# Feed-forward down products of the middle steps in pairs of 64-row matmuls

## The chip, the cores and the metric

One core of a Trainium2 chip runs the whole program. The metric is device time in microseconds (us) of one execution, as the median over the runs shown. The core has a matmul engine (TensorE, PE in the profile, with its weight loads shown apart as PEld), a vector engine (DVE), a scalar engine (ACT), GpSimd (POOL) and queues that issue DMAs.

## The reference, cut to what matters

Two transformer blocks follow each other on 256 tokens of width 1024, all in fp32. They hold five feed-forward parts (swiglu), one in the first block and four in the second:

```
def _swiglu(h, w_gate_up, w_down):
    g, u = jnp.split(h @ w_gate_up, 2, axis=-1)
    return (jax.nn.silu(g) * u) @ w_down
```

The hidden width is 2816, so that the down product sums over 2816 hidden features for each of the 256 x 1024 outputs.

## The kernel before, in words

All products run on TensorE in fp32r, a rounded form of fp32. To keep accuracy each operand is held as a high and a low part (whi and wlo of the weights, st_hi and st_lo or hid_hi and hid_lo of the activations), and `product` (lines 661 to 665) makes three matmuls of each: high x high, high x low, low x high, all added in one PSUM bank. A matmul is written `128*128 128x512` in the profile: 128 rows (the summed dimension) and 128 columns of the stationary operand, then the moving operand with its 512 columns.

Weights come in units of 128 x 2048. A DMA puts a unit into `raw`, ACT rounds it into `whi` (line 1415), DVE subtracts to get `wlo` (line 1984), and TensorE uses it; each of the three buffers is a ring of three. TensorE counts the units that it has finished in `w_used`, and ACT waits for that count before it fills a place again.

`swiglu` on TensorE (line 1042) takes the hidden width in FSTEPS = 11 steps of 256 features. A step has three units: two for gate and up, one for down. The order on TensorE is the gate and up products of step i (`gate_up`, 48 matmuls into banks 4 and 5), then the down products of step i-1 (`down`, line 1083). Meanwhile ACT and DVE make silu, the hidden values and their turned and split form `hid_hi` and `hid_lo`, 128 features by 2 by 256 tokens. `down` waits for `hid_ready` and for its weight unit, and calls `down_block` (line 1069) for each of two token blocks tb. A block loops over two output halves h and two feature groups f; each (tb, h) has its own bank, and all eleven steps add to the same four banks 0 to 3. A step has 2 x 2 x 2 x 3 = 24 down matmuls, each 128*128 with 512 moving columns.

`down` runs for steps 0 to 8 of each feed-forward part: once before the loop (line 1106) and eight times in `pe.Fori` (line 1107). Steps 9 and 10 are written out after the loop and call `down_block` themselves. So `down` runs 9 x 5 = 45 times in the program.

The kernel has other matmuls that use 64 rows: `scores2` (line 1254) in the second attention computes heads in pairs, the even head on rows 0 to 63 and the odd one on rows 64 to 127, in plain fp32, where the profile shows two matmul instructions for each call. Its semaphore `even_scored` (lines 1253 and 1259) keeps two halves off one bank. `cmp_scores` (line 1273) does the same with 16 moving columns. `values2` (lines 1320 to 1330) uses 64 stationary columns. The product for the attention gates ("g2") is in fp32r with 48 stationary columns.

Of the kernel before, what the change touches and what calls it, by code (L numbers as in the profile page):

```python
# [30 lines left out]
P = 128  # L31
# [5 lines left out]
FSTEPS = DFF // FC  # L37
# [40 lines left out]
def build(nc, A, out):  # L78
    ctx = ExitStack()
    with ctx:  # L80
        def sb(name, shape, dt=F32):
            return ctx.enter_context(nc.sbuf_tensor(name, shape, dt))

        def sem(name):
            return ctx.enter_context(nc.semaphore(name))
# [9 lines left out]
        hid_hi = sb("hid_hi", [P, 2, S], F32R)  # L95
        hid_lo = sb("hid_lo", [P, 2, S], F32R)
# [127 lines left out]
        w_used = sem("w_used")  # L224
# [28 lines left out]
        factor_ready = sem("factor_ready")  # L253
        factor1_ready = sem("factor1_ready")
        even_scored = sem("even_scored")
        prob_end_ready = sem("prob_end_ready")
        cmp_p_ready = sem("cmp_p_ready")
        act_step = sem("act_step")
# [93 lines left out]
        def at(base, i=0):  # L352

            return base + RING * i, base % RING, base // RING + i
# [143 lines left out]
        def bank(key):  # L498
            return ps[:, use[key][0], :]
# [15 lines left out]
        def is_full(key):  # L515
            return bank_full[use[key][0]], 1
# [137 lines left out]
        def _(pe):  # L654
# [6 lines left out]
            def product(o, a, b, start, stop):  # L661

                pe.matmul(o, a[0], b[0], start=start, stop=False)  # L663
                pe.matmul(o, a[0], b[1], start=False, stop=False)  # L664
                return pe.matmul(o, a[1], b[0], start=False, stop=stop)  # L665
# [163 lines left out]
            for h in range(2):  # L829
                pe.matmul(gain_rows(h), ones, gb[0:1, 1, 512 * h:512 * h + 512], start=True,  # L830
                          stop=True).then_inc(gain_ready, 1)
# [12 lines left out]
                      stop=True).then_inc(*is_full("rows"))  # L844
            room("kidx")
            u = first["kidx"]
            features(u, [(0, bank("kidx")[:, 0:S])]).then_inc(w_used, 1)
            room("qidx")
            u = first["qidx"]
# [3 lines left out]
            for tb in range(2):  # L853
                mm = pe.transpose(bank("widx")[:, 4 * tb:4 * tb + 4], widxT[64:68, tb * P:tb * P + P],
                                  ident[64:68, 64:68])
            mm.then_inc(*is_full("widx"))
            room("kv")
            u = first["kv"]
# [5 lines left out]
            for j in range(2):  # L864
                mm = pe.matmul(bank(("dots", 0))[:, S * j:S * j + S].rearrange("p (a b) -> p a b", a=2),
                               qidx[:, j, 0:P], kidx[:, :, 0:P], start=True, stop=True)
            mm.then_inc(*is_full(("dots", 0)))
            for j in range(2):
                room(("dots", 1 + j))
                pe.matmul(bank(("dots", 1 + j)), qidx[:, j, P:2 * P], kidx[:, :, :].rearrange("p a b -> p (a b)"),  # L870
                          start=True, stop=True).then_inc(*is_full(("dots", 1 + j)))
# [12 lines left out]
            for tb in range(2):  # L884
                mm = pe.transpose(bank("vT")[:, tb * P:tb * P + P], v1T[:, tb * P:tb * P + P], ident)
# [8 lines left out]
            for j in range(2):  # L894
                room(("pool", j))
                for g in (2 * j, 2 * j + 1):
                    src = (winA, winB)[g % 2]
                    mm = pe.matmul(bank(("pool", j))[:, (g % 2) * S:(g % 2 + 1) * S], poolw[:, g, :],
                                   src[:, g, 16:272], start=True, stop=True)
# [142 lines left out]
            def swiglu(n, name=None, src=None, ahead=None, middle=None, behind=None, between=None):  # L1042
                u0 = first["ffn", n]
                up = [("up", n, tb) for tb in range(2)]
                ykeys = [[("y", ("ffn", n), tb, h) for h in range(2)] for tb in range(2)]

                def gate_up(i, base, j, between=None):
                    for half in range(2):
                        u, s, _ = at(base + half, j)
                        pe.wait_ge(wlo_ready, u + 1)  # L1050
                        w = [x[:, s, :].rearrange("p (k c) -> p k c", k=4) for x in (whi, wlo)]
                        for tb, key in enumerate(up):
                            if half == 0:

                                b, c = use[key]
                                pe.wait_ge(bank_read[b], c + i)
                            for k in range(4):
                                mm = product(bank(key), [x[:, 4 * half + k, tb * P:tb * P + P] for x in (st_hi, st_lo)],
                                             [x[:, k, :] for x in w], half == 0 and k == 0, half == 1 and k == 3)
                            if half == 1 and tb == 0:  # L1060
                                mm.then_inc(*is_full(up[0]))
                        mm.then_inc(w_used, 1)
                        if half == 0 and between is not None:
                            between()

                def down_block(w, x_hi, x_lo, tb, start=False, end=False, ahead=None):
                    for h in range(2):
                        for f in range(2):
                            if ahead is not None and (h, f) == (1, 1):
                                ahead()  # L1070
                            mm = product(bank(ykeys[tb][h]), [x[:, f, tb * P:tb * P + P] for x in (x_hi, x_lo)],
                                         [x[:, f, 512 * h:512 * h + 512] for x in w], start and f == 0,
                                         end and f == 1)
                        if end and (tb, h) != (1, 1):
                            mm.then_inc(*is_full(ykeys[tb][h]))
                    return mm

                def down_weights(base, j):
                    u, s, _ = at(base, j)
                    pe.wait_ge(wlo_ready, u + 1)  # L1080
                    return [x[:, s, :].rearrange("p (k c) -> p k c", k=2) for x in (whi, wlo)]

                def down(i, base, j, start=False):

                    pe.wait_ge(hid_ready, hid_count(n, i))
                    w = down_weights(base, j)
                    down_block(w, hid_hi, hid_lo, 0, start)
                    down_block(w, hid_hi, hid_lo, 1, start).then_inc(w_used, 1)

                def turn_last(tb):  # L1090
                    key = ("hid_last", n, tb)
                    pe.wait_ge(*read(up[tb], FSTEPS - 1))
                    room(key)
                    for f in range(2):
                        mm = pe.transpose(bank(key)[:, f * P:f * P + P], hidden[:, tb, f * P:f * P + P], ident)
                    mm.then_inc(*is_full(key))

                by_block([(u0 + half, 4, 512, 4 * half, [bank(key) for key in up], up, half == 0, half == 1)
                          for half in range(2)], st=name, src=src, middle=middle)
                if behind is not None:  # L1100
                    behind()

                gate_up(1, u0 + 2, 0, between=between)
                for key in (k for pair in ykeys for k in pair):
                    room(key)
                down(0, u0 + 4, 0, start=True)
                with pe.Fori(2, FSTEPS - 1) as i:
                    gate_up(i, u0 + 2, i - 1)
                    down(i - 1, u0 + 4, i - 1)


                i = FSTEPS - 1
                gate_up(i, u0 + 2, i - 1)
                turn_last(0)
                pe.wait_ge(hid_ready, hid_count(n, i - 1))
                w_before = down_weights(u0 + 4, i - 1)
                down_block(w_before, hid_hi, hid_lo, 0)
                turn_last(1)
                w_last = down_weights(u0 + 3 * FSTEPS - 1, 0)
                last = [x[:, 8:10, :] for x in (st_hi, st_lo)]  # L1120
                pe.wait_ge(*read(("hid_last", n, 0)))
                down_block(w_last, *last, 0, end=True)
                down_block(w_before, hid_hi, hid_lo, 1).then_inc(w_used, 1)
                pe.wait_ge(*read(("hid_last", n, 1)))
                down_block(w_last, *last, 1, end=True, ahead=ahead).then_inc(w_used, 1)
# [8 lines left out]
            for j in range(2):  # L1134
                room(("wsT", j))
                for q in range(4):
                    mm = pe.transpose(bank(("wsT", j))[:, q * P:q * P + P], ws[:, 4 * j + q, :], ident)
                mm.then_inc(*is_full(("wsT", j)))
            for j in range(2):
                room(("bs", j))  # L1140
                for q in range(4):
                    v = vec[:, V_BS + 4 * j + q:V_BS + 4 * j + q + 1]
                    mm = pe.matmul(bank(("bs", j))[:, q * P:q * P + P], view(v, (0, P)), ident, start=True, stop=True)
# [79 lines left out]
            w = weights(first["g2"], KD, 48)  # L1223
            for k in range(KD):
                if k % 4 == 0:
                    wait_st("ln3", k // 4)
                mm = product(bank("g2")[0:48, 0:S], [x[:, k, :] for x in w], [x[:, 8 + k, :] for x in (st_hi, st_lo)],
                             k == 0, k == KD - 1)
# [108 lines left out]
            for g in range(4):  # L1337
                for f in range(2):
                    mm = pe.matmul(bank("vc")[:, g * 64:g * 64 + 64], cmp_gr[:, f, g, :],
                                   cmp_w2[:, 1, f, 0:64], start=f == 0, stop=f == 1)  # L1340
# [3 lines left out]
            for tb in range(2):  # L1344
                mm = pe.transpose(bank("g2T")[:, 48 * tb:48 * tb + 48], gateT2[0:48, tb * P:tb * P + P],
                                  ident[0:48, 0:48])
# [1619 lines left out]
```

## Time and profile before

| what | value |
|---|---|
| median of 2 runs | 1455.52 us (1455.5 to 1455.54) |
| the profiled execution, its own time | 1458.33 us |
| its span, first to last instruction | 1456.6 us |
| around the span | 1.7 us |
| granted TensorE clock, mean | 0.998 |

The profiled execution is 0.2% longer than the median of the runs shown. PE busy time counts overlapping instructions once, and an instruction's own time holds its way through the array too: back to back matmuls of 0.39 us start 0.23 us apart. What counts for throughput is the distance between starts.

### The profile page before, as it was taken

The numbers are of one execution on the slowest core, as the hardware profiler recorded it, in microseconds if no ns is written. First come the engines' busy times: TensorE is split into PE (matmuls) and PEld (weight loads), VectorE is DVE, ScalarE is ACT, GpSimd is POOL, SyncE is SP. The second block draws the span as 40 slices with busy tenths as digits, with TensorE's granted clock in tenths as the row PEclk, the third lists the DMA queues.
The fourth block names the chain that finished last, engine by engine and source line by source line (L and its number), as shares of the span: only waits on it lengthen the run. The fifth ranks groups of instructions, "written<-read, shape, count | busy, mean of one in ns | idle before, by whom it ended". The sixth has DMA issues, their size and how long they took to land.

```text
span 1456.6 us, 20700 instructions
## 1 busy us (share of the span) xinstructions
PE 1438.3 (99%) x7418; PEld 1210.3 (83%) x7418; DVE 1077.1 (74%) x1818; ACT 679.2 (47%) x848; POOL 207.4 (14%) x191
## 2 busy tenths in 40 slices
PE   9999999999999999999999999999999999999997
PEld 7988897888888888889988888888888897788886
DVE  5666766888777887757758887757877777688876
ACT  5346456444444444443434444435444477454342
POOL 1073011200001000300032000201000325510001
PEclk9999999999999999999999999999999999999999
DMA  8753553865656556575577555775556450465561
GB/s 251 255 174 126 203 178 117 295 209 173 198 193 206 197 173 198 177 231 173 169 236 240 201 173 194 238 231 173 173 196 207 150 174 30 139 236 174 183 215 64
DMA packets 198701, 273.94 MB, mean 188 GB/s; under 512 B 9585, under 2 KB 158193, under 8 KB 198386
## 3 DMA queue, kind: packets, MB, share of 16 engines
q1 hardware_dynamic: 194130, 256.10, 53.6%
q0 software_dynamic: 4368, 16.78, 3.2%
q8 instruction: 39, 0.64, 0.2%
q10 hardware_dynamic: 144, 0.26, 0.0%
q14 instruction: 20, 0.16, 0.0%
HBM read 271.80 MB, written 1.31 MB: 187 GB/s over the span
## 4 chain that ended last, share of the span: by engine, by line
PE 90%; DVE 3%; POOL 3%; ACT 2%; issue 1%; DVEq 0%; ACTq 0%; POOLq 0%
PE ps L663 25%; PE ps L665 25%; PE ps L664 25%; PE ps L775 3%; PE ps L758 3%; PE ps L769 3%; PE ps L704 1%; POOL wlo L2747 1%; ACT whi L1415 1%; PE ps L1153 0%; PE ps L1189 0%; PE ps L1254 0%; DVE big L2571 0%; DVE wlo L1984 0%; POOL big L2793 0%
## 5 line engine op out<-in xcount | busy, mean ns | idle before, releaser
L1984 DVE TENSOR_TENSOR wlo<-raw,whi 128x2048 fp32r<-128x2048 f32 (+1 forms) x221 | 502.5, 2291 | 169.1 <-ACT whi L1415 167.2
L1415 ACT CAST whi<-raw 128x2048 fp32r<-128x2048 f32 (+1 forms) x236 | 447.1, 1895 | 375.3 <-PE ps L665 327.6
L663 PE MATMUL ps<-whi,st_hi 128*128 128x512 f32 x1048 | 410.3, 392 | 0.0
L665 PE MATMUL ps<-whi,st_lo 128*128 128x512 f32 x1048 | 408.0, 389 | 0.0
L664 PE MATMUL ps<-wlo,st_hi 128*128 128x512 f32 x1048 | 407.9, 389 | 0.0
L2398 DVE STREAM_TRANSPOSE hidT<-hidden 32x128 f32<-32x128 f32 x800 | 242.2, 303 | 12.3
L665 PEld LDWEIGHTS ps<-whi,st_lo 128*128 128x128 f32 x1048 | 196.7, 188 | 40.9
L663 PEld LDWEIGHTS ps<-whi,st_hi 128*128 128x128 f32 x1048 | 196.8, 188 | 40.6 <-issue 0.3
L664 PEld LDWEIGHTS ps<-wlo,st_hi 128*128 128x128 f32 x1048 | 196.8, 188 | 40.4
L663 PE MATMUL ps<-whi,hid_hi 128*128 128x512 f32 x400 | 156.1, 390 | 0.0
L665 PE MATMUL ps<-whi,hid_lo 128*128 128x512 f32 x400 | 155.7, 389 | 0.0
L664 PE MATMUL ps<-wlo,hid_hi 128*128 128x512 f32 x400 | 155.6, 389 | 0.0
L2747 POOL TENSOR_TENSOR wlo<-raw,whi 128x2048 fp32r<-128x2048 f32 x15 | 69.4, 4629 | 573.7 <-ACT whi L1415 573.7
L663 PE MATMUL ps<-st_hi,whi 128*128 128x256 f32 (+1 forms) x464 | 133.2, 287 | 0.0
L664 PE MATMUL ps<-st_lo,whi 128*128 128x256 f32 (+1 forms) x464 | 131.2, 283 | 0.0
L665 PE MATMUL ps<-st_hi,wlo 128*128 128x256 f32 (+1 forms) x464 | 131.2, 283 | 0.0
L1688 ACT ACTIVATE silu<-ps 128x256 f32<-128x256 f32 x110 | 42.2, 384 | 154.2 <-PE ps L665 150.2
L2387 DVE TENSOR_TENSOR hidden<-ps,silu 128x256 f32<-128x256 f32 x110 | 46.0, 421 | 73.9 <-ACT silu L1688 73.9
L663 PEld LDWEIGHTS ps<-st_hi,whi 128*128 128x128 f32 (+1 forms) x464 | 88.4, 190 | 1.5 <-issue 1.2
L664 PEld LDWEIGHTS ps<-st_lo,whi 128*128 128x128 f32 (+1 forms) x464 | 88.4, 191 | 0.7 <-issue 0.5
L665 PEld LDWEIGHTS ps<-st_hi,wlo 128*128 128x128 f32 (+1 forms) x464 | 88.4, 190 | 0.0
L664 PEld LDWEIGHTS ps<-wlo,hid_hi 128*128 128x128 f32 x400 | 75.1, 188 | 15.6
(262 smaller groups left out, 1426.2 us busy)
## 6 DMA issues: line engine op xcount, KB each, us to landing
raw<-in_ffn_w SPq DMA_DIRECT2D x264, 512.0 KB, 4.9
raw<-in_w_gate_up SPq DMA_DIRECT2D x44, 512.0 KB, 4.8
raw<-in_w_in SPq DMA_DIRECT2D x32, 512.0 KB, 4.8
raw<-in_sgu_w_in SPq DMA_DIRECT2D x32, 512.0 KB, 4.7
raw<-in_w_down SPq DMA_DIRECT2D x22, 512.0 KB, 5.2
raw<-in_sgu_w_out SPq DMA_DIRECT2D x16, 512.0 KB, 4.8
raw<-in_kv_w SPq DMA_DIRECT2D x12, 512.0 KB, 4.7
raw<-in_w_proj_attn SPq DMA_DIRECT2D x8, 512.0 KB, 4.5
```

Source lines behind the costliest of these rows:

```text
L663: pe.matmul(o, a[0], b[0], start=start, stop=False)
L664: pe.matmul(o, a[0], b[1], start=False, stop=False)
L665: return pe.matmul(o, a[1], b[0], start=False, stop=stop)
L758: pe.matmul(outs[tb], st_hi[:, k0 + k, t], w_hi[:, k, :], start=start and k == 0, stop=False)
L769: pe.matmul(outs[tb], st_hi[:, k0 + k, t], w_lo[:, k, :], start=False, stop=False)
L775: mm = pe.matmul(outs[tb], st_lo[:, k0 + k, t], w_hi[:, k, :], start=False, stop=stop and k == kt - 1)
L1415: act.copy(whi[:, s, 0:n], raw[:, s, 0:n]).then_inc(whi_ready, 1)
L1688: act.activation(silu[:, tb, :], bank(("up", n, tb))[:, 0:FC], ACT.Silu).then_inc(silu_ready, 1)
L1984: dve.tensor_tensor(wlo[:, s, 0:n], raw[:, s, 0:n], whi[:, s, 0:n].bitcast(F32), ALU.subtract).then_inc(wlo_ready, 1)
L2387: dve.tensor_tensor(hidden[:, tb, :], bank(("up", n, tb))[:, FC:2 * FC], silu[:, tb, :], ALU.mult).then_inc(*is_read(("up", n, tb)))
L2398: mm = dve.transpose(dst, src)
L2747: pool.tensor_tensor(wlo[:, s, 0:n], raw[:, s, 0:n], whi[:, s, 0:n].bitcast(F32), ALU.subtract).then_inc(wlo_ready, 1)
```

## The change

`down` calls a new function `row_pairs` in place of `down_block` twice. Each 128-row matmul becomes two matmuls of 64 rows, on rows 0 to 63 and 64 to 127, with the same 128 stationary and 512 moving columns: 48 in place of 24. Two matmuls that follow each other form a pair, one on each half of the rows, and add to different banks. In the first phase the lower rows add to the banks of token block 0 and the upper rows to those of block 1; in the second phase they change over. Between the phases TensorE waits on the new semaphore `rows_done`, which the last matmul of the first phase raises. Ahead of the first phase there is a wait for `w_used` of unit u-2, the one that the last down product of the step before has raised.

```
+        rows_done = sem("rows_done")
...
+                def row_pairs(w, x_hi, x_lo, start, u, count):
+
+                    outs = [(tb, h) for tb in range(2) for h in range(2)]
+                    pe.wait_ge(w_used, u - 2)
+                    for phase in range(2):
+                        if phase:
+                            pe.wait_ge(rows_done, count)
+                        for f in range(2):
+                            for x, y in ((x_hi, 0), (x_hi, 1), (x_lo, 0)):
+                                for j in range(2):
+                                    for r in (0, 64):
+                                        tb, h = outs[(2 * phase + j + (2 if r else 0)) % 4]
+                                        mm = pe.matmul(bank(ykeys[tb][h]), x[r:r + 64, f, tb * P:tb * P + P],
+                                                       w[y][r:r + 64, f, 512 * h:512 * h + 512],
+                                                       start=start and (phase, f, x is x_hi, y) == (0, 0, True, 0),
+                                                       stop=False)
+                        if phase == 0:
+                            mm.then_inc(rows_done, 1)
+                    return mm
...
-                    down_block(w, hid_hi, hid_lo, 0, start)
-                    down_block(w, hid_hi, hid_lo, 1, start).then_inc(w_used, 1)
+                    row_pairs(w, hid_hi, hid_lo, start, at(base, j)[0],
+                              (FSTEPS - 2) * n + i + 1).then_inc(w_used, 1)
```

## Rows read from the trace of the kernel before

**Rows 1.** The page, busy time and the 40 slices.
```profile
PE 1438.3 (99%) x7418; PEld 1210.3 (83%) x7418; DVE 1077.1 (74%) x1818; ACT 679.2 (47%) x848; POOL 207.4 (14%) x191
PEclk9999999999999999999999999999999999999999
```

**Rows 2.** The page, chain that ended last, by engine and by line.
```profile
PE 90%; DVE 3%; POOL 3%; ACT 2%; issue 1%; DVEq 0%; ACTq 0%; POOLq 0%
```

**Rows 3.** The page, groups of instructions: count, busy us, mean ns.
```profile
L663 PE MATMUL ps<-whi,hid_hi 128*128 128x512 f32 x400 | 156.1, 390 | 0.0
...
L665 PE MATMUL ps<-whi,hid_lo 128*128 128x512 f32 x400 | 155.7, 389 | 0.0
L664 PE MATMUL ps<-wlo,hid_hi 128*128 128x512 f32 x400 | 155.6, 389 | 0.0
```

**Rows 4.** Windows over the feed-forward loops: stretch, length, busy us of PE first.
```profile
271.00:424.00 153.00, 153.00 (x678) 126.58 (x677) 121.74 (x205) 65.37 (x60) 1.10 (x1) 1.00 0.65 217
...
424.00:601.00 177.00, 177.00 (x789) 1.00 0.58 191
...
1290.00:1436.00 146.00, 146.00 (x646) 1.00 0.57 193
```

**Rows 5.** Waits, longest first: who waited for TensorE's products.
```profile
ACT whi L1415 <- PE ps L665: 327.6, 107, 5.2
```

**Rows 6.** Timeline of PE around one down step: start us, us.
```profile
404.03 0.39 PE L665 MATMUL ps<-whi,st_lo 128*128 128x512 f32 x1
404.26 0.39 PE L663 MATMUL ps<-whi,hid_hi 128*128 128x512 f32 x1
404.49 0.39 PE L664 MATMUL ps<-wlo,hid_hi 128*128 128x512 f32 x1
...
409.47 0.39 PE L665 MATMUL ps<-whi,hid_lo 128*128 128x512 f32 x1
409.70 0.39 PE L663 MATMUL ps<-whi,st_hi 128*128 128x512 f32 x1
```

**Rows 7.** Timeline of PE, 64-row pairs of line 1254 between fp32r products.
```profile
1202.81 0.28 PE L664 MATMUL ps<-st_lo,whi 128*128 128x256 f32 x1
1202.93 0.28 PE L665 MATMUL ps<-st_hi,wlo 128*128 128x256 f32 x1
1203.14 1.56 PE L1254 MATMUL ps<-big 64*128 64x256 f32 x8
1204.63 0.39 PE L663 MATMUL ps<-st_hi,whi 128*128 128x256 f32 x1
1204.86 0.28 PE L664 MATMUL ps<-st_lo,whi 128*128 128x256 f32 x1
```

**Rows 8.** Plain fp32 on all 128 rows: timeline of line 870 and its source view.
```profile
43.35 1.88 PE L870 MATMUL ps<-big 128*128 128x512 f32 x4
...
L870 PE MATMUL ps<-big x4: 592/592/592, 43.3 to 44.6; 128*128 128x512 f32 x4
```

**Rows 9.** Timeline of PEld and PE inside the block of rows 7.
```profile
1203.46 0.19 PEld L1254 LDWEIGHTS ps<-big 64*128 64x128 f32 x1
...
1203.68 0.19 PEld L1254 LDWEIGHTS ps<-big 64*128 64x128 f32 x1
...
1203.89 0.18 PEld L1254 LDWEIGHTS ps<-big 64*128 64x128 f32 x1
...
1204.33 0.38 PE L1254 MATMUL ps<-big 64*128 64x256 f32 x1
```

**Rows 10.** Timeline of PEld: weight loads that matmuls of few columns don't cover.
```profile
1179.38 0.64 PEld L1339 LDWEIGHTS ps<-big 128*128 128x128 f32 x5
...
1189.04 1.86 PEld L1273 LDWEIGHTS ps<-big 64*128 64x128 f32 x31 [0.24 <-issue]
```

**Rows 11.** Source view of the wait in line 1085, on PE's sequencer.
```profile
L1085 PEldq ALU_OP  x32: 32/32/32, 468.0 to 1417.3; - x32
L1085 PEldq EVENT_SEMAPHORE  x5: 51/51/51, 271.9 to 1289.1; - x5
```

**Rows 12.** Timeline of PE: fp32r goes to 48 columns; then fp32 to 64.
```profile
1169.64 0.28 PE L665 MATMUL ps<-st_hi,wlo 128*128 128x256 f32 x1
1169.76 0.28 PE L663 MATMUL ps<-st_hi,whi 128*48 128x256 f32 x1
...
1207.49 0.28 PE L665 MATMUL ps<-st_hi,wlo 128*128 128x256 f32 x1
1207.70 0.65 PE L1320 MATMUL ps<-tmp,big 128*64 128x256 f32 x4
```

## The prediction

> **What bounds the kernel now.** I read the page first. TensorE is busy 99% of the span, DVE 74%, and the granted clock is at its upper level throughout, 2.4 GHz [rows 1]. The chain that ended last lies on PE for 90% [rows 2]. A share of busy time can hide gaps, so I looked at the feed-forward loops by windows: PE is busy for every microsecond of them, 153.00 of 153.00 us in the first and likewise in the others, at clock 1.00 [rows 4]. The waits say the same from the other side: the largest wait of ACT in these loops is for TensorE, 327.6 us over 107 times [rows 5]. Whatever the change adds to TensorE's time in a step is added to the kernel, and no other engine's slack pays for it.
>
> The timeline of one step gives the unit of account. The first down matmul starts at 404.26, the first of the next gate and up product at 409.70: 24 matmuls in 5.44 us, 0.227 us each [rows 6], though each is 0.39 us long [rows 3]. 512 columns at 2.4 GHz are 0.213 us, so a matmul carries 0.0135 us of its own. 45 such steps are 245 us, which is what the change touches: 45 x 24 = 1080 of the 1200 matmuls in [rows 3].
>
> **The change, part by part.**
>
> *No column is saved.* A 64-row matmul still streams 512 columns. 48 of them are 24 pair times, and a pair can't be shorter than one stream of 512 columns, 0.213 us against 0.227. All that can be won is 24 x 0.0135 = 0.32 us a step, 15 us or 1% of the kernel, before any cost.
>
> *Do the two of a pair run beside each other?* The kernel already has such pairs, in plain fp32, at line 1254. One block of 8 instructions has four with 512 columns and four with 256. On the full array a 512-column instruction of this kind takes (1.88 - 0.59) / 3 = 0.43 us from start to start [rows 8], so one after the other the block would be 4 x 0.43 + 4 x 0.215 = 2.58 us. It takes 1.56 us with the tail of the last, and the next product starts 1.49 us after its beginning [rows 7]. Half of 2.58 is 1.29: they run in pairs. I carry this over to fp32r.
>
> *Weight loads* double to 48. Where matmuls are too short to cover them, a load on the full array takes (0.64 - 0.19) / 4 = 0.11 us, and on 64 rows (1.86 - 0.19) / 30 = 0.056 us, that is two at once, one on each half [rows 10]. A pair of loads is 0.11 us and lies under a pair of matmuls of over 0.21 us. Cost nothing; without that cover, it would be 24 x 0.11 = 2.6 us a step.
>
> *The time of a pair* in fp32r is not in the trace. Lower end: 0.216, as the 64-row fp32 instructions step (weight loads at 1203.46, 1203.68, 1203.89: 0.215 each for the same 512 cycles) [rows 9]. Upper end with the pair still together: both halves pay the other's 0.0135 too, 0.240. I take 0.227, because the nearest row in type and column rate is the fp32r one [rows 6]. So the pairs cost +0 a step, from -0.26 to +0.31.
>
> By the Trainium skill ("TensorE: Matmul & The Clock Gate", section "Back-to-back issue gap") an isolated warm matmul steps at N/2.4 + 2.5 ns, 216 ns for 512 columns; by that the pairs would give back 0.26 us a step, and the whole sum below would be 12 us less. This case's fp32r rows step 227 ns and don't follow it; its 64-row fp32 rows do.
>
> *Going into and out of the 64-row mode.* Around the block of line 1254, from the last fp32r matmul at 1202.93 to the second one after at 1204.86 are 1.93 us [rows 7]. Two ordinary steps of 0.12 (1202.81 to 1202.93) and 1.29 of paired streaming leave 0.40 us. One sees where it is: the block starts 0.21 after the last matmul in place of 0.12 and its first weight load isn't covered; at the end the next load starts 0.30 after the last matmul's start [rows 9], and its matmul is 0.39 long in place of 0.28. A step of the changed kernel goes in and out once: +0.40. Lower end nothing (the second rival), upper end 0.50, with two register operations and a semaphore instruction more on the sequencer, 0.03 and 0.05 [rows 11], if the drain doesn't hide them.
>
> *The wait between the phases.* Everything behind it on TensorE stands: 24 matmuls, then the next gate and up product, for which ACT and DVE wait. The same kind of wait exists at line 1253. The matmul that raises it begins at 1203.46 (each load in this block starts as a matmul begins), is 0.38 long, and the load that waits starts at 1203.89, 0.43 later [rows 9]. For a matmul of 0.39 that is 0.44; then the uncovered load, 0.11, makes 0.55 to the next stream in place of 0.227: +0.32. Lower end 0.19, if the release came as early as at the block's end (0.30 + 0.11 - 0.227); upper end 0.40 with the sequencer's 0.08.
>
> *The wait for w_used* is for the unit of the step before, and 48 matmuls of gate and up, 10.9 us, lie between: nothing. The place of the down unit in the ring comes free 0.7 us later, but is needed again only after the next 48 matmuls, and refilling takes one cast and one subtraction, some 4 us. The same holds for hid_hi and hid_lo. Banks 4 and 5 get more time to be read. DMAs are the same, on the same queues.
>
> *Sum:* 0.40 + 0.32 + 0 = 0.72 us a step, 45 steps: +32 us. On the profiled execution 1458.3 + 32 = 1491; its span has the same 1.7 us around it. The median of the runs shown is 2.8 us below it, so I predict 1488 us, 2.2% above. A measurement here can tell about 2% from no change, 29 us, so the line lies at 1484.6.
>
> **Rivals.**
>
> *The pairs don't pair (the change doesn't do what it says).* fp32r may hold the whole array, so that the 48 run one after the other: 24 x 0.227 = 5.45 us more a step, with 0.32 for the wait and none or 0.40 for the mode: 5.8 to 6.2 us, 260 to 278 us, 1715 to 1733. For it: fp32r with 48 stationary columns follows the full array after 0.12 us, with no break, whereas fp32 with 64 columns starts 0.21 later and runs in pairs [rows 12]; so fp32r isn't split by columns. Against it: the split by rows uses all columns, and two halves of the rows have different weights and inputs. The Trainium skill ("PSUM — Partial Sum Buffer", section "The four PSUM rules") says that float32r matmuls force the whole column group; it says nothing on row groups, and the 48-column rows agree.
>
> *No drain for fp32r.* The same rows read the other way: if a 64-row fp32r matmul needs no change of mode, the 0.40 goes and only the wait stays, 0.32 x 45 = 14 us: 1470, and 1458 if pairs also step at 0.216. This ends on the other side: within 2%. It decides as soon as in and out together are under 0.32 us a step. Against it: in pairs each half must be fed by itself, and [rows 7] show a drain at each side of such a block.
>
> *Cheaper or dearer pairs.* At 0.216: 0.46 a step, 21 us, 1476. At 0.240: 1.03 a step, 46 us, 1502.
>
> **How the numbers follow.** The forecast, drain and wait with pairs near 0.227: 0.43, spread some 6 us around 1488, so 0.30 above 1484.6 and 0.13 below. Pairs at 0.216: 0.15. Pairs at 0.240: 0.12. No drain: 0.15. No pairing: 0.13. Faster by over 2% would need 29 us of a possible 15; 0.02 for what I don't see. Slower: 0.30 + 0.12 + 0.13 = 0.55; same: 0.13 + 0.15 + 0.15 = 0.43. The range from 1466 to 1505 holds the first three and most of the no-drain case; left out are no pairing, and no drain with cheap pairs.
>
> **What would show it.** In the profile after: 120 in place of 400 matmuls in each group of [rows 3], and 2160 of form 64*128 64x512, whose starts come two by two within some ns and 0.227 from pair to pair; a down step of about 6.2 us from its first matmul to the next gate and up one; one gap of 0.55 in its middle; its first pair some 0.2 late and the gate and up one after it too; PE still without idle time named for another engine. Single starts 0.22 apart would mean no pairing; no gap at the edges, no drain. If DVE, ACT or a DMA is named before TensorE's work in these loops, my reading of the slack is wrong.

## The result, and the profile after

The changed kernel takes 1496.04 us (median of 2 runs, 1494.82 to 1497.26) against 1455.52: a ratio of 1.0278, 95% interval 1.0234 to 1.0323. A second measurement, after_again below, gave 1.0271 (1.0254 to 1.0288). It is slower by about 40 us. Runs of both kernels come out mostly at one of two times some 2.5 us apart (before near 1456 or 1458.2, after near 1494.8 or 1497.5), and like against like the difference is 39 us. The forecast of 1488 us had the direction and the range (1466 to 1505), and was 8 us too low.

The page of the kernel after, busy time of the engines, the granted clock, then the groups of the new line 1091:

```profile
PE 1471.9 (99%) x8498; PEld 1199.1 (80%) x8498; DVE 1076.9 (72%) x1818; ACT 678.9 (45%) x848; POOL 206.9 (14%) x191
...
PEclk9999999999999999999999999999999999999999
...
L1091 PE MATMUL ps<-whi,hid_hi 64*128 64x512 f32 x720 | 121.9, 416 | 2.8
L1091 PE MATMUL ps<-wlo,hid_hi 64*128 64x512 f32 x720 | 113.1, 392 | 0.0
...
L1091 PE MATMUL ps<-whi,hid_lo 64*128 64x512 f32 x720 | 111.0, 386 | 0.0
```

TensorE has 33.6 us more busy time than in [rows 1], in an execution 36.5 us longer than the profiled one of before (1494.82 against 1458.33), with 1080 matmuls more (8498 against 7418) and the same clock. The 2160 new ones are about as long as those of [rows 3]; the 416 ns hold the first pairs behind a break, which are 0.1 longer. A share of busy time, 99% before and after, doesn't show that anything happened; the timeline does. PE in the kernel after, one down step (start us, us; x4 are two pairs):

```profile
408.45 0.39 PE L666 MATMUL ps<-whi,st_lo 128*128 128x512 f32 x1
408.76 0.73 PE L1091 MATMUL ps<-whi,hid_hi 64*128 64x512 f32 x4
409.33 0.63 PE L1091 MATMUL ps<-wlo,hid_hi 64*128 64x512 f32 x4
409.80 0.62 PE L1091 MATMUL ps<-whi,hid_lo 64*128 64x512 f32 x4
...
411.19 0.61 PE L1091 MATMUL ps<-whi,hid_lo 64*128 64x512 f32 x4
411.86 0.73 PE L1091 MATMUL ps<-whi,hid_hi 64*128 64x512 f32 x4
412.43 0.63 PE L1091 MATMUL ps<-wlo,hid_hi 64*128 64x512 f32 x4
...
414.28 0.61 PE L1091 MATMUL ps<-whi,hid_lo 64*128 64x512 f32 x4
414.82 0.50 PE L664 MATMUL ps<-whi,st_hi 128*128 128x512 f32 x1
415.16 0.40 PE L665 MATMUL ps<-wlo,st_hi 128*128 128x512 f32 x1
415.39 0.40 PE L666 MATMUL ps<-whi,st_lo 128*128 128x512 f32 x1
415.63 0.40 PE L664 MATMUL ps<-whi,st_hi 128*128 128x512 f32 x1
```

Behind the first row of a phase, four matmuls, two pairs, start every 0.46 to 0.47 us: the pairs do run beside each other. Against [rows 6] one sees three breaks. Going in, the first pair starts 0.31 after the last full matmul in place of 0.227, and the 0.73 holds 0.11 for a weight load that nothing covers. Between the phases the last pair (the second half of the row at 411.19, starting at 411.41) is followed at 411.86, and again 0.11 is uncovered. Going out, the next full matmul is 0.50 long in place of 0.39.

The whole step shows the price. PE in the kernel before and then in the kernel after, the first down matmul of the step ahead of the one in [rows 6] and of the one above:

```profile
387.94 0.39 PE L663 MATMUL ps<-whi,hid_hi 128*128 128x512 f32 x1
...
391.58 0.50 PE L1091 MATMUL ps<-whi,hid_hi 64*128 64x512 f32 x2
```

From there to the next step are 16.32 us before (to 404.26) and 17.18 after (to 408.76): 0.86 more, 39 us in 45 steps.

The weight loads (PEld) name what ended the second break, and the source view of line 1091 how often:

```profile
411.86 0.30 PEld L1091 LDWEIGHTS ps<-whi,hid_hi 64*128 64x128 f32 x4 [0.49 <-PE ps L1091]
...
  PE ps L1091: 21.8, 45
  issue: 15.8, 45
```

45 times TensorE's loads stood still for its own matmuls, 0.48 us each, and 45 times at the way in, 0.35 us each. ACT waits for TensorE as before:

```profile
ACT whi L1436 <- PE ps L666: 201.2, 65, 5.2
ACT whi L1436 <- PE ps L1091: 165.4, 43, 3.9
```

Together 366.6 us against 327.6 in [rows 5], 39 us more: the other engines only waited longer.

What the forecast had not: the pairs step at 0.231 and not 0.227 (from 408.87, where the first stream begins, to 411.41 are eleven of them), and the full matmuls behind the block start 0.23 to 0.24 apart at first (415.16, 415.39, 415.63). The question for the runs: do half-row pairs cost something by themselves, or does each restart?

### The profile page after: what moved, and what is told of

It reads as the page before. It is cut to its first block, busy times and chain, and to the rows that moved or that the text cites. A ratio compares the mean times of both kernels' runs of the same rounds, so it can differ in the third digit from the quotient of the medians.

```text
span 1493.1 us, 22932 instructions
## 1 busy us (share of the span) xinstructions
PE 1471.9 (99%) x8498; PEld 1199.1 (80%) x8498; DVE 1076.9 (72%) x1818; ACT 678.9 (45%) x848; POOL 206.9 (14%) x191
## 4 chain that ended last, share of the span: by engine, by line
PE 90%; DVE 3%; POOL 3%; ACT 2%; issue 1%; DVEq 0%; ACTq 0%; POOLq 0%
PE ps L664 20%; PE ps L666 19%; PE ps L665 19%; PE ps L1091 18%; PE ps L776 3%; PE ps L759 3%; PE ps L770 3%; PE ps L705 1%; POOL wlo L2768 1%; ACT whi L1436 1%; PE ps L1174 0%; PE ps L1210 0%; PE ps L1275 0%; DVE big L2592 0%; DVE wlo L2005 0%
## 5 line engine op out<-in xcount | busy, mean ns | idle before, releaser
L664 PE MATMUL ps<-whi,st_hi 128*128 128x512 f32 x1048 | 416.4, 397 | 0.0
L1091 PE MATMUL ps<-whi,hid_hi 64*128 64x512 f32 x720 | 121.9, 416 | 2.8
L1091 PE MATMUL ps<-wlo,hid_hi 64*128 64x512 f32 x720 | 113.1, 392 | 0.0
L1091 PE MATMUL ps<-whi,hid_lo 64*128 64x512 f32 x720 | 111.0, 386 | 0.0
L1091 PEld LDWEIGHTS ps<-whi,hid_hi 64*128 64x128 f32 x720 | 60.7, 185 | 44.9 <-PE ps L1091 21.8
```

The lines of the kernel that those rows point to most:

```text
L1091: mm = pe.matmul(bank(ykeys[tb][h]), x[r:r + 64, f, tb * P:tb * P + P], w[y][r:r + 64, f, 512 * h:512 * h + 512], start=start and (phase, ...
```

## The experiments

A restart is the first matmul behind a break; the run-in is the stretch of slower steps behind it. Theory A: a restart costs its break and then a slow run-in of some 0.05 us; half-row pairs themselves cost nothing. Theory B: half-row pairs in fp32r step at 0.231. Theory C: the breaks aren't where the time goes.

**e1_order**: the change-over of the halves waits for pairs that ended long ago.

```
 for phase in range(2):
-    if phase:
-        pe.wait_ge(rows_done, count)
-    for f ...: for x, y ...: for j in range(2): for r in (0, 64): ...
-    if phase == 0:
-        mm.then_inc(rows_done, 1)
+    for j in range(2):
+        if phase:
+            pe.wait_ge(rows_done, count + j)
+        for f ...: for x, y ...: for r in (0, 64): ...
+        if phase == 0:
+            mm.then_inc(rows_done, 1)
```

> The same 48 half-row matmuls a step, but the output half is now the outer loop: six pairs per bank before the halves change over, so that each change-over waits for pairs that ended six pairs, some 1.4 us, earlier. Theory A (each restart of TensorE costs its bubble, 0.33 us at this wait, and then some 0.05 us over the next eleven matmuls until they step at 0.227 again; 64-row pairs as such step at 0.227): the bubble and one of the slow runs-in go, 0.38 us x 45 = 17 us below the changed kernel, 1479 us; pairs 12 to 23 of a step 0.227 apart. Theory B (64-row fp32r pairs step at 0.231 by themselves): only the bubble goes, 0.33 x 45 = 15 us, 1481 us, and all pairs stay 0.231 apart. Theory C (the wait costs nothing, the loss is elsewhere): 1496 us.

Measured: 1479.47 us, ratio to before 1.0148 (1.0131 to 1.0165). A's 1479 and B's 1481 are too near for the time to tell; the timeline tells. PE in e1_order, one step from its beginning, its middle and its end:

```profile
408.74 0.40 PE L1091 MATMUL ps<-whi,hid_lo 64*128 64x512 f32 x2
408.97 0.40 PE L1091 MATMUL ps<-whi,hid_hi 64*128 64x512 f32 x2
409.21 0.39 PE L1091 MATMUL ps<-wlo,hid_hi 64*128 64x512 f32 x2
...
411.05 0.39 PE L1091 MATMUL ps<-whi,hid_hi 64*128 64x512 f32 x2
...
413.54 0.39 PE L1091 MATMUL ps<-whi,hid_lo 64*128 64x512 f32 x2
413.86 0.50 PE L664 MATMUL ps<-whi,st_hi 128*128 128x512 f32 x1
```

The break in the middle is gone, and from 411.05 to 413.54 eleven pairs take 2.49 us, 0.226 each, as full matmuls do. Before that they still run in, mostly 0.23 to 0.24. Theory B falls. e1_order leaves nothing out and is 17 us faster than the changed kernel, yet slower than the one before. A second measurement gave the same:

> The same kernel as e1_order, on the same chip as e5_stay, so that the two can be compared: 1479 us, and 4 us above e5_stay by theory A.

Measured: 1480.38 us, ratio 1.0149 (1.0132 to 1.0166). The second part of that expectation, 4 us above e5_stay, failed; see there.

**e2_wait**: the full matmuls of before, with the wait alone.

```
-    down_block(w, hid_hi, hid_lo, 0, start)
+    down_block(w, hid_hi, hid_lo, 0, start).then_inc(rows_done, 1)
+    pe.wait_ge(rows_done, (FSTEPS - 2) * n + i + 1)
     down_block(w, hid_hi, hid_lo, 1, start).then_inc(w_used, 1)
```

> The kernel before, 24 matmuls on all 128 rows, with nothing added but the wait in the middle of each of the 45 steps. Theory A: bubble 0.33 and a slow run-in of 0.05 a step, 17 us above before, 1472 us; the matmuls behind the wait start 0.235, 0.233, 0.236 apart before they settle at 0.227. Theory B: 0.33 x 45 = 15 us, 1470 us, and 0.227 from the first matmul on. Theory C: 1456 us.

Measured: 1473.45 us, ratio 1.0111 (1.0094 to 1.0128), 14 to 19 us. PE in e2_wait around the wait:

```profile
407.12 0.39 PE L666 MATMUL ps<-whi,hid_lo 128*128 128x512 f32 x1
407.56 0.50 PE L664 MATMUL ps<-whi,hid_hi 128*128 128x512 f32 x1
407.90 0.40 PE L665 MATMUL ps<-wlo,hid_hi 128*128 128x512 f32 x1
408.14 0.40 PE L666 MATMUL ps<-whi,hid_lo 128*128 128x512 f32 x1
...
410.23 0.39 PE L666 MATMUL ps<-whi,hid_lo 128*128 128x512 f32 x1
```

Break: 0.44 and 0.11 uncovered, less 0.227: 0.32. Run-in: from 407.90 to 410.23 ten matmuls take 2.33 us where 2.27 would do, 0.06 more. Nothing here uses 64 rows, so break and run-in belong to the wait.

**e3_one_pair**: the change of mode alone, on the kernel before. In place of the first product of two outputs one pair stands at the front of a step; the other half of the rows of these two products is left out.

```
+    for tb, r in ((0, 0), (1, 64)):
+        pe.matmul(bank(ykeys[tb][0]), hid_hi[r:r + 64, 0, tb * P:tb * P + P],
+                  w[0][r:r + 64, 0, 0:512], start=start, stop=False)
+    ... the other 22 matmuls of the step on all rows
```

> The kernel before, but two of the 24 matmuls of a step are replaced by one 64-row pair at the front; no wait is added. Left out: one half of the rows in each of these two products. So a step goes into the 64-row mode and out again once, with 23 matmul times in place of 24. Theory A (the change of mode costs 0.39 us whatever lies between, and the run-in behind it 0.05): 0.39 + 0.05 - 0.23 = 0.21 us a step, 45 steps, 10 us above before, 1465 us. If the gaps at the edges were due to the semaphore waits there and not to the mode: 0.23 x 45 = 10 us below before, 1445 us.

Measured: 1466.23 us, ratio 1.0057 (1.0041 to 1.0074), 6 to 11 us above before. PE in e3_one_pair:

```profile
405.52 0.39 PE L665 MATMUL ps<-whi,st_lo 128*128 128x512 f32 x1
405.84 0.50 PE L1088 MATMUL ps<-whi,hid_hi 64*128 64x512 f32 x2
406.27 0.50 PE L1094 MATMUL ps<-wlo,hid_hi 128*128 128x512 f32 x1
406.61 0.40 PE L1094 MATMUL ps<-whi,hid_lo 128*128 128x512 f32 x1
406.84 0.39 PE L1094 MATMUL ps<-whi,hid_hi 128*128 128x512 f32 x1
```

From 405.52 to the second full matmul at 406.61 are 1.09 us; three ordinary steps would be 0.68. In and out cost 0.41, with no wait added, so the breaks at the edges are those of the mode. The run-in is only 0.02 here; why it is shorter than the 0.05 of other restarts is open.

**e4_one_half**: both matmuls of a pair on rows 0 to 63; the upper 64 rows of the sums are left out and the lower counted twice.

```
-    x[r:r + 64, f, ...], w[y][r:r + 64, f, ...]
+    x[0:64, f, ...], w[y][0:64, f, ...]
```

> The changed kernel, but both matmuls of a pair work on rows 0 to 63, so nothing can lie beside it. The upper 64 rows of the sums are left out and the lower counted twice. If the pairs of the changed kernel really run beside each other and a 64-row matmul alone takes as long as a full one: 24 more matmul times a step, 24 x 0.227 x 45 = 245 us, less the slow run-in that then covers a smaller part, about 1738 us. If 64 rows alone are quicker than 128: less than that, and matmuls less than 0.227 apart.

Measured: 1739.47 us, one run. PE in e4_one_half:

```profile
412.84 1.07 PE L1091 MATMUL ps<-wlo,hid_hi 64*128 64x512 f32 x4
413.75 1.06 PE L1091 MATMUL ps<-whi,hid_lo 64*128 64x512 f32 x4
```

Four in 0.91 us, 0.227 each: a matmul on 64 rows alone takes what one on 128 rows takes. The 243 us between this and the changed kernel show that its pairs share their time, and what the first rival (no pairing) would have cost; I had put it at 1715 to 1733.

**e5_stay**: no change of mode in the loops, by giving gate and up products the same pairs.

```
 with pe.Fori(2, FSTEPS - 1) as i:
-    gate_up(i, u0 + 2, i - 1)
+    gate_up_pairs(i, u0 + 2, i - 1, count)   # unit 1, unit 2; rows_done; unit 1, unit 2 turned over
     down(i - 1, u0 + 4, i - 1)
```

> On top of e1_order the gate and up products of the eight looped steps of each feed-forward part run as 64-row pairs too (lower rows to bank 4 and upper rows to bank 5, then changed over behind one wait on rows_done); the down product of step 0 is on the full array again. So in the loops TensorE never leaves the 64-row mode: 5 changes in and out in place of 45, and 40 uncovered waits. Theory A (the cost is the changes of mode and the restarts, pairs themselves are free): 40 x (0.33 + 0.05) + 5 x 0.49 = 18 us above before, 1474 to 1476 us, some 4 us below e1_order, and no gap between down and gate and up products. If 64-row pairs cost anything of their own, three times as many of them show it: 0.004 us for each of 72 pairs a step would add 12 us, 1487 us. If the gaps at the edges of the down products come from the change of operands or banks and not of the mode, they stay: 1479 + 15 = 1494 us. Silu of the first token block can start only 2.7 us later than before; if ACT or DVE then come late, the profile names them as what TensorE waits for.

Measured: 1542.79 us, ratio 1.0588 (1.057 to 1.0605): 67 us over what A gives. The breaks at the edges of the down products were gone, but a new one came. Waits of PE, then its timeline around the beginning of a step, in e5_stay:

```profile
PE ps L1096 <- DVE wlo L2037: 55.5, 37, 1.9
...
298.88 0.39 PE L1096 MATMUL ps<-whi,st_lo 64*128 64x512 f32 x2
300.79 0.50 PE L1096 MATMUL ps<-whi,st_hi 64*128 64x512 f32 x2 [1.52 <-DVE wlo L2037]
```

The first pair on the second weight unit starts 1.91 us after the pair before it, in place of 0.227: 1.7 us a step, 67 us in 40 steps. My order did two things to the weights. It held the first unit until 36 of 72 pair times of a step had passed, not 24, so that its place in the ring was refilled later; and it asked for the second unit after 12 pair times, not 24. The expectation had named ACT and DVE, but because of silu. In e6_halves silu comes as late and the mode is the same, so it tells those from the order of the weights.

**e6_halves**: the same, ordered by weight unit.

```
-    unit 1, unit 2; wait; unit 1 turned over, unit 2 turned over
+    unit 1; wait; unit 1 turned over, unit 2 turned over; wait; unit 2
```

> e5_stay with the gate and up products ordered by weight unit: both parts of the first unit, then both parts of the second in turned order, so that the first unit is released after 24 pair times, as in the kernel before, and not after 36. Price: two uncovered waits a step in place of one. If the 1.9 us a step that e5_stay waited for DVE come from the late release, they go: 40 x 2 x 0.38 + 5 x 0.49 = 33 us above before, 1489 to 1491 us, 52 us below e5_stay, and no wait for DVE in the loops. If DVE is late for another reason (silu of both token blocks coming late, or the 64-row mode itself), some 1.9 us a step stay: 1560 us or more.

Measured: 1490.09 us, ratio 1.0225 (1.0208 to 1.0242), as worked out, and the waits of PE name no engine in the loops. PE in e6_halves, from the second wait of one step through the down products to the first wait of the next:

```profile
304.67 0.39 PE L1096 MATMUL ps<-whi,st_lo 64*128 64x512 f32 x2
305.12 0.49 PE L1096 MATMUL ps<-whi,st_hi 64*128 64x512 f32 x2
...
307.76 0.39 PE L1096 MATMUL ps<-whi,st_lo 64*128 64x512 f32 x2
307.99 0.39 PE L1118 MATMUL ps<-whi,hid_hi 64*128 64x512 f32 x2
...
313.20 0.39 PE L1118 MATMUL ps<-whi,hid_lo 64*128 64x512 f32 x2
313.43 0.39 PE L1096 MATMUL ps<-whi,st_hi 64*128 64x512 f32 x2
...
315.92 0.39 PE L1096 MATMUL ps<-whi,st_lo 64*128 64x512 f32 x2
316.37 0.49 PE L1096 MATMUL ps<-whi,st_hi 64*128 64x512 f32 x2
```

The 24 pairs of the down products, 307.99 to 313.43, take 5.44 us, to the hundredth what 24 full matmuls take in [rows 6], and at both their edges there is no gap. Only the two waits show, 305.12 and 316.37. With mode and waits away, half-row pairs are as fast as full rows, and no faster.

So neither silu nor the mode made DVE late in e5_stay; the order of the weights did. DVE in e5_stay, then in e6_halves:

```profile
292.58 0.75 DVE L2440 TENSOR_TENSOR hidden<-ps,silu 128x256 f32<-128x256 f32 x2
...
298.45 4.49 DVE L2037 TENSOR_TENSOR wlo<-raw,whi 128x2048 fp32r<-128x2048 f32 x2
...
308.60 0.76 DVE L2439 TENSOR_TENSOR hidden<-ps,silu 128x256 f32<-128x256 f32 x2 [1.99 <-ACT silu L1740]
...
314.47 4.49 DVE L2036 TENSOR_TENSOR wlo<-raw,whi 128x2048 fp32r<-128x2048 f32 x2
```

In both, DVE subtracts the second unit (the first half of the x2) only behind the hidden values. It is ready 4.3 us into the step in e5_stay, whose first pair starts at 296.39, and 3.3 us in e6_halves (313.43). In e5_stay the hidden values start 1.63 us after the first down pair (290.95), because DVE is still subtracting the late first unit; in e6_halves they start 0.61 after it (307.99). Asked for after 12 pair times, 2.7 us, the unit would be late even at 3.3; asked for after 24, 5.4 us, it would not be late even at 4.3. So by these rows the early asking made TensorE wait, and the late release made the wait longer, by about 1.0 of the 1.7 us. No run shows the two apart: e6_halves turns both back.

**after_again**: the changed kernel beside e6_halves.

> The changed kernel itself, beside e6_halves on the same chip: 1496 us, 2.8% above before.

Measured: 1497.52 us, ratio 1.0271 (1.0254 to 1.0288).

No version beat the kernel before: with the changes of mode and the waits out of the way, the down products of a step take the 5.44 us that they had.

## Why the prediction was right, and where it was short

*What bounds it*: right. All that TensorE lost was added to the kernel's time: 0.86 us in each of 45 steps is 39 us. The waits of PE after name no other engine in these loops, and ACT's wait grew by 39 us.

*No column is saved, pairs pair, loads are covered*: right, shown by e4_one_half and by the 0.226 of e1_order. The first rival fell, and with it what it drew from the 48-column rows [rows 12]: fp32r wasn't split by columns there, but is split by rows here. One of the signs was miscounted: 40 full matmuls are left in each group of [rows 3], not 120, which is what the three groups have together.

*Going in and out, +0.40*: right; 0.41 in e3_one_pair, which also fells the second rival (no drain). The row of a plain fp32 block [rows 7] carried over to fp32r. e1_order has the wait for w_used, which e3_one_pair has not, and its ways in and out (407.85 to 408.50 and 413.54 to 414.19, each 0.65 for two steps of 0.227) cost 0.39, so that wait costs nothing, as forecast.

*The wait, +0.32*: right; 0.32 in e2_wait. (Its lower end is 0.18 by its own terms, not 0.19.)

*Pairs at 0.227, +0*: the step that was mis-sized. Steady pairs do take 0.227, but after each restart of the changed kernel the first eleven or so take longer together by about 0.05, and a phase of twelve pairs never gets beyond that. A step of the changed kernel has three restarts: 11 pairs at 0.231 twice (22 x 0.0043 = 0.095) and the run-in of the gate and up products (0.05). 0.72 + 0.145 = 0.865 a step, as the 0.86 of the whole step shows; x 45 = 39 us, against 40.5 between the medians and 39 like against like. So the 0.231 lay within the bounds for the pair (0.216 to 0.240), but for another reason than the two I had: neither the other half's 0.0135 nor a cheaper step. The trace of before had it, and I had read only the settled stretch. PE in the kernel before, behind a transposition at the end of a loop, with starts 0.23 to 0.24 apart:

```profile
424.03 0.40 PE L664 MATMUL ps<-wlo,st_hi 128*128 128x512 f32 x1
424.26 0.40 PE L665 MATMUL ps<-whi,st_lo 128*128 128x512 f32 x1
424.50 0.40 PE L663 MATMUL ps<-whi,st_hi 128*128 128x512 f32 x1
```

By the Trainium skill ("TensorE: Matmul & The Clock Gate", section "Back-to-back issue gap") I had weighed 216 ns for a pair; the measured 226 to 227 in e1_order and e6_halves, as in the full-array rows, don't agree with that.

The account closes from the other side as well: e1_order takes away one break and one run-in and gives 17 us; what is left of it over before, 21.5 us by its ratio, is 45 x (0.40 + 0.05 + 0.05) = 22.5.

## What to carry to other kernels

Splitting a full 128-row fp32r product of 512 columns into half-row pairs won nothing here: a pair takes what one full matmul takes, 0.227 us. What it adds is a break and an uncovered weight load at each change of mode (0.4 us for in and out), a break wherever TensorE waits for its own last matmul (0.32), and a run-in behind each (0.02 to 0.06). e1_order hid the second by ordering the work so that something else lies between; e6_halves was rid of the first in its loops by staying in the mode. If you reorder to stay, watch when each buffer is released and when the next one is asked for: e5_stay lost 67 us by moving both by 2.7 us.

## What the runs showed that was not expected

Behind the way into the 64-row mode, fp32r matmuls of 512 columns start 0.235, 0.233, 0.236, 0.224, 0.231, 0.236, 0.228, 0.232, 0.231 us apart before they step at 0.227: 0.046 us in all. The same order comes on full rows (behind the wait of e2_wait, with a step of 0.240 ahead of it: 0.06), on half-row pairs (the changed kernel; behind its wait the first step is 0.229: 0.04) and on one half alone (the way into e4_one_half). It is not always that long: in e3_one_pair, and at the other two restarts of a step of e4_one_half, it begins only at the 0.236 before 0.228, or one step ahead of it, and costs 0.02. What makes it, and what sets its length, was not tried.
